# First operands by k over two queues, a bias wait at its first use, and another order around the last block's x1 and the sums

## The reference

```
h = rmsnorm(x, norm_mix_g)
z = gelu(h @ a_w_in);  u, v = split(z, 2)
v = rmsnorm(v, a_v_g)
s = per chunk of 128 tokens and group of 128 features: tril(w_s) @ v + b_s
x = x + (u * s) @ a_w_out
a = relu(rmsnorm(x, norm_mlp_g) @ mlp_w1)      # 4096 wide
x = x + (a * a) @ mlp_w2
out = rmsnorm(x, final_g)
```

## Time and profile before

| | |
|---|---|
| median of 3 runs | 1824.14 us (1823.81 to 1824.42) |
| the profiled execution | 1827.29 us |
| its span | 1825.5 us |
| busy, share of the span: PE, PEld, DVE, ACT, POOL | 99%, 82%, 61%, 43%, 22% |
| mean granted clock of TensorE | 0.996 |

### The profile page before, as it was taken

The page is one execution under the profiler, slowest core; times in us unless marked ns, Lnnn a source line. Parts: engine busy times, 40 slices in busy tenths (PEclk is TensorE's granted clock), DMA queues, the critical chain, the costliest instruction groups (busy, mean ns, idle before and its releaser), DMA issues.

```text
span 1825.5 us, 20165 instructions
## 1 busy us (share of the span) xinstructions
PE 1802.2 (99%) x8136; PEld 1497.9 (82%) x8136; DVE 1111.1 (61%) x1122; ACT 782.5 (43%) x880; POOL 407.1 (22%) x394
## 2 busy tenths in 40 slices
PE   9999999999999899999999999999999999999998
PEld 7888888888888788888878888878888888888886
DVE  3583483484384566654666655685666666866665
ACT  5553544434534533444543443354433335333333
POOL 2442442432340133310002111110234002000002
PEclk9999999999999899999999999999999999999999
DMA  8757656665655588875957777799977555854552
GB/s 329 269 209 267 240 215 241 244 244 204 234 199 201 199 290 267 303 263 183 355 197 237 259 256 229 278 367 319 309 299 264 220 202 201 288 184 185 199 205 103
DMA packets 134157, 445.40 MB, mean 244 GB/s; under 512 B 8112, under 2 KB 9136, under 8 KB 118320
## 3 DMA queue, kind: packets, MB, share of 16 engines
q1 hardware_dynamic: 105728, 329.02, 51.3%
q0 software_dynamic: 25168, 92.80, 14.3%
q10 hardware_dynamic: 3168, 22.30, 3.2%
HBM read 318.26 MB, written 125.83 MB: 243 GB/s over the span
## 4 chain that ended last, share of the span: by engine, by line
PE 92%; DVE 2%; DMA 2%; ACT 1%; SPq 1%; issue 1%; DVEq 0%; POOLq 0%; POOL 0%; ACTq 0%
PE bank L1263 62%; PE bank L1098 28%; DMA u_raw<-in_mlp_w 1%; PE bank L1144 1%; PE bank L1120 1%; SPq L312 1%; DMA bias_rows<-in_a_b_s 1%; PE bank L1147 0%; DMA x_raw<-xs 0%; DVE Y L1036 0%; ACT x_hi L581 0%; DVE x_lo L849 0%; DVE r L1017 0%; DVE sums L1020 0%; DVE u_lo L838 0%
## 5 line engine op out<-in xcount | busy, mean ns | idle before, releaser
L1263 PE MATMUL bank<-x_hi,u_hi 128*128 128x512 f32 x896 | 351.0, 392 | 8.0 <-ACT c L755 4.8
L1263 PE MATMUL bank<-x_lo,u_hi 128*128 128x512 f32 x896 | 349.9, 391 | 0.0
L1263 PE MATMUL bank<-x_hi,u_lo 128*128 128x512 f32 x896 | 349.8, 390 | 0.0
L1263 PE MATMUL bank<-d_lo,a_hi 128*128 128x512 f32 x896 | 348.9, 389 | 0.0
L1263 PE MATMUL bank<-d_hi,a_hi 128*128 128x512 f32 x896 | 348.9, 389 | 0.0
L1263 PE MATMUL bank<-d_hi,a_lo 128*128 128x512 f32 x896 | 348.9, 389 | 0.0
L838 DVE TENSOR_TENSOR u_lo<-u_raw,u_hi 128x1024 fp32r<-128x1024 f32 x112 | 148.9, 1329 | 180.2 <-ACT u_hi L571 180.2
L1007 DVE TENSOR_TENSOR Y<-bank,Y 128x512 f32<-128x512 f32 x208 | 138.0, 686 | 179.8 <-PE bank L1263 179.6
L576 ACT ACTIVATE d_hi<-d_raw 128x2048 fp32r<-128x2048 f32 x56 | 107.4, 1919 | 282.2 <-DMA d_raw<-w2sum 153.7
L832 DVE TENSOR_TENSOR w_lo<-w_raw,w_hi 128x2048 fp32r<-128x2048 f32 x47 | 116.5, 2490 | 171.5 <-ACT w_hi L566 160.5
L1263 PEld LDWEIGHTS bank<-x_hi,u_hi 128*128 128x128 f32 x896 | 168.9, 189 | 45.6 <-issue 8.4
(11 more groups left out here) (113 smaller groups left out, 2763.3 us busy)
## 6 DMA issues: line engine op xcount, KB each, us to landing
a_raw<-a2s SPq DMA_DIRECT2D x56, 1024.0 KB, 7.3
a2s<-sums SPq DMA_DIRECT2D x32, 1280.0 KB, 7.9
job<-in_mlp_w POOLq DMA_DIRECT2D x32, 1024.0 KB, 8.2
u_raw<-w1sum SPq DMA_DIRECT2D x64, 512.0 KB, 4.7
d_raw<-w2sum SPq DMA_DIRECT2D x32, 1024.0 KB, 4.9
w_raw<-in_a_w_in SPq DMA_DIRECT2D x31, 1024.0 KB, 5.9
u_raw<-in_mlp_w SPq DMA_DIRECT2D x48, 512.0 KB, 5.4
d_raw<-in_mlp_w SPq DMA_DIRECT2D x24, 1024.0 KB, 5.2
```

The source lines that it names most:

```text
L1263: ins = pe.matmul(bank_of(g, j)[:, :], stationary[x_part][:, k, j * P:(j + 1) * P], moving[y_part][:, k, :], start=i in (0, 1, 3) and k == ...
```

## The change

Unit 0's weights and the first four k-tiles of hT are loaded k by k, the weights on SP's queue, hT on ACT's (the gains behind the first k-tile); ACT, DVE and TensorE take them k by k. The warm-up has 44 transposes. DVE waits for the bias in the first `gate`. In ACT's loop `renew` comes before `finish_first` at i = 6, and behind `keep_x1T` at g = 4 and 5; the squares of the last x1 come at g = 1 behind `renew` instead of g = 0. DVE does `finish_second` for j = 0 at i = 0 in front of `renew`, and for j = 1 at i = 2 behind it, and SP stores these sums at i = 2 and 4. The other lines of the diff renumber semaphores, since unit 0 no longer counts in `w_hi_done`, `w_ready` and `w_loaded`.

```diff
-WARM = 48
+WARM = 44
...
-            for k in range(0, KU, 2):
-                rows = slice(k, k + 2)
-                to = (first_loaded[0], w_loaded[0])[k // 2]
-                sp.dma_start(w_raw[0][:, rows, :], w_in_v[:, rows, D:D + N]).then_inc(to, 16)
-                to = (first_loaded[1], xT_loaded[0])[k // 2]
-                sp.dma_start(hT_raw[0][:, rows, :], xT[0, 0][:, rows, :]).then_inc(to, 16)
+            for k in range(KU):
+                sp.dma_start(w_raw[0][:, k, :], w_in_v[:, k, D:D + N]).then_inc(first_w_loaded[k], 16)
...
-                if g >= STEPS and g % STEPS in (0, 1, 3, 5):
-                    part, j = {0: (0, 0), 1: (0, 1), 3: (1, 0), 5: (1, 1)}[g % STEPS]
+                if g >= STEPS and g % STEPS in (0, 1, 2, 4):
+                    part, j = {0: (0, 0), 1: (0, 1), 2: (1, 0), 4: (1, 1)}[g % STEPS]
...
-                    if q == 0 and k < 2:
-                        act.wait_ge(first_loaded[1], 16)
+                    if q == 0 and k < KU:
+                        act.wait_ge(first_h_loaded[k], 16)
                     else:
-                        act.wait_ge(xT_loaded[k // KU], 16 * (q + 1))
+                        act.wait_ge(xT_loaded[k // KU], 16 * (q if k < KU else q + 1))
...
+            act.dma_start(hT_raw[0][:, 0, :], xT[0, 0][:, 0, :]).then_inc(first_h_loaded[0], 16)
             act.dma_start(gains[:, :, :], gains_T).then_inc(gains_loaded, 16)
+            for k in range(1, KU):
+                act.dma_start(hT_raw[0][:, k, :], xT[0, 0][:, k, :]).then_inc(first_h_loaded[k], 16)
 
             act.wait_ge(half_done, 2)
             act.activation(junk[:, 0:2 * TT], minus_half[:, :], ACT.Copy).then_inc(warm, 1)
-            act.wait_ge(first_loaded[0], 16)
-            act.activation(w_hi[0][:, 0:2, :], w_raw[0][:, 0:2, :], ACT.Copy).then_inc(first_hi_done, 1)
-            act.wait_ge(gains_loaded, 16)
-            split_h(0, range(2))
-            act.wait_ge(w_loaded[0], 16)
-            act.activation(w_hi[0][:, 2:KU, :], w_raw[0][:, 2:KU, :], ACT.Copy).then_inc(w_hi_done, 1)
-            split_h(0, range(2, KD))
+            for k in range(KU):
+                act.wait_ge(first_w_loaded[k], 16)
+                act.activation(w_hi[0][:, k, :], w_raw[0][:, k, :], ACT.Copy).then_inc(first_hi_done, 1)
+                if k == 0:
+                    act.wait_ge(gains_loaded, 16)
+                split_h(0, range(k, k + 1))
+            split_h(0, range(KU, KD))
...
                     if i == 6:
+                        renew(g)
                         for j in range(2):
                             finish_first(c, j)
                     if i in (0, 2, 3, 6):
...
                             act.wait_ge(second_half, 6 * 2 * c)
                         for j in range(2):
                             keep_bank(g, j, to[:, j, :], ACT.Relu if i == 6 else ACT.Copy)
-                    renew(g)
-                    if g == 0:
-                        squares_x1(BLOCKS - 1)
                     if g == 4:
                         keep_x1T(BLOCKS - 1, 0)
                     if g == 5:
                         keep_x1T(BLOCKS - 1, 1)
+                    if i < 6:
+                        renew(g)
+                    if g == 1:
+                        squares_x1(BLOCKS - 1)
...
+                if q == 0 and g == 0:
+                    dve.wait_ge(bias_loaded, 16)
...
-            dve.wait_ge(first_hi_done, 1)
-            dve.tensor_tensor(w_lo[0][:, 0:2, :], w_raw[0][:, 0:2, :], f32(w_hi[0][:, 0:2, :]), ALU.subtract)\
-                .then_inc(first_ready, 1)
-            dve.wait_ge(gains_loaded, 16)
-            split_h(0, range(2))
-            dve.wait_ge(w_hi_done, 1)
-            dve.tensor_tensor(w_lo[0][:, 2:KU, :], w_raw[0][:, 2:KU, :], f32(w_hi[0][:, 2:KU, :]), ALU.subtract)\
-                .then_inc(w_ready, 1)
-            split_h(0, range(2, KD))
+            for k in range(KU):
+                dve.wait_ge(first_hi_done, k + 1)
+                dve.tensor_tensor(w_lo[0][:, k, :], w_raw[0][:, k, :], f32(w_hi[0][:, k, :]), ALU.subtract)\
+                    .then_inc(first_ready, 1)
+                if k == 0:
+                    dve.wait_ge(gains_loaded, 16)
+                split_h(0, range(k, k + 1))
+            split_h(0, range(KU, KD))
             split_w(1)
-            dve.wait_ge(bias_loaded, 16)
...
-                if c and i in (2, 3):
-                    finish_second(c - 1, i - 2)
+                if c and i == 0:
+                    finish_second(c - 1, 0)
                 renew(g)
+                if c and i == 2:
+                    finish_second(c - 1, 1)
...
-                if w == 0:
-                    pe.wait_ge(first_ready, 1)
-                else:
-                    pe.wait_ge(w_ready, w + 1)
+                if w:
+                    pe.wait_ge(w_ready, w)
                 for k in range(KU):
-                    if w == 0 and k == 2:
-                        pe.wait_ge(w_ready, 1)
+                    if w == 0:
+                        pe.wait_ge(first_ready, k + 1)
```

More of the change, by code:

```diff
@@ L175, in build @@
         mix_done, x1T_done = sem("mix_done"), sem("x1T_done")
-        first_loaded = [sem("first_w_loaded"), sem("first_h_loaded")]
+        first_w_loaded = [sem(f"first_w_loaded{k}") for k in range(KU)]
+        first_h_loaded = [sem(f"first_h_loaded{k}") for k in range(KU)]
         warm = sem("warm")
@@ L564, in split_w @@
             def split_w(w):
-                act.wait_ge(w_loaded[w % SLOTS], 16 * (w // SLOTS + 1))
+                act.wait_ge(w_loaded[w % SLOTS], 16 * (w // SLOTS + (1 if w % SLOTS else 0)))
                 act.activation(w_hi[w % SLOTS][:, :, :], w_raw[w % SLOTS][:, :, :], ACT.Copy)\
@@ L830, in split_w @@
                 s = w % SLOTS
-                dve.wait_ge(w_hi_done, w + 1)
+                dve.wait_ge(w_hi_done, w)
                 dve.tensor_tensor(w_lo[s][:, :, :], w_raw[s][:, :, :], f32(w_hi[s][:, :, :]), ALU.subtract)\
@@ L836, in split_u @@
                 s = g % SLOTS
[L837 removed]
+                dve.wait_ge(w_hi_done, FIRST + g)
                 dve.tensor_tensor(u_lo[s][:, :, :], u_raw[s][:, :, :], f32(u_hi[s][:, :, :]), ALU.subtract)\
@@ L1244, in _ @@
                     b = g // (UP // PAIRS * STEPS)
-                    pe.wait_ge(w_ready, FIRST + g + 1)
+                    pe.wait_ge(w_ready, FIRST + g)
                     pe.wait_ge(a_ready, b * STEPS + i + 1)
```

3 lines of the change are left out of this document (1 added, 2 removed).

## The result

| | before | after |
|---|---|---|
| median | 1824.24 us (4 runs, 1823.81 to 1824.42) | 1810.32 us (4 runs, 1809.70 to 1811.35) |
| ratio, with its 95% interval | | 0.9928 [0.9915, 0.9940] |
| the profiled execution | 1827.29 us | 1810.33 us |
| its span | 1825.5 us | 1808.6 us |
| mean granted clock of TensorE | 0.996 | 0.999 |

The kernel is faster by 13.9 us, 0.72%. Forecast were 19.1 us and 1805.0; the ratio puts the kernel at 1811.0 (0.9928 x 1824.14), the upper edge of the range. Between the two profiled executions it is 16.9 us. The interval is 2.3 us wide to either side, and those of the experiments are of that order.

What follows compares the result with a forecast made beforehand. TensorE was taken as the bound, with a few breaks: 2.35 + 11.1 + 0.45 + 4.45 + 1.75 = 20.1 us at most, less 1.0 for margins, 19.1; 1824.14 - 19.1 = 1805.0 us, range 1803.5 to 1811.

Steps and rivals of the forecast that it cites:

- The five places: The five breaks in TensorE's work that the change was to remove, together 20.1 us at most.
- Place 2: Steps 2 to 5 of the second stage (593.47 to 618.12): 10.25 us, with faster matmuls behind it 11.1 us.
- Places 3 and 5: Step 26 (733.37 to 733.81), 0.45 us, and steps 107 to 111 (1179.54 to 1203.08), 1.75 us: both losses go.
- the difference is applied to the median: Last step of the sum: 19.1 us, worked out on the profiled execution, taken from the median 1824.14 to give 1805.0.
- Place 1: First unit and bias wait (start to 32.80): unit 2 starts 2.15 us earlier, with slow first matmuls 2.35 us gained.
- behind a transfer that has the same bytes in front of it as before: Unit 1's w_lo, written from 17.26 to 19.55 as before, so unit 1 starts at 19.7 and not 20.23: 0.5 us.
- TensorE free at 8.55: End of the warm-up: four transposes less save 0.44 us, so TensorE is free at 8.55 instead of 8.98.
- Rival D: First unit starves: half-size pieces in two queues arrive later, unit 0 stops at each k; 1806 to 1809, chance 0.04.
- Place 4: Steps 54 to 61 (886.43 to 929.02): 4.45 us lost, all regained, or 2.4 if u_raw(57) lands no earlier.
- Rival C: DVE's full queue in steps 54 to 61 keeps 2.4 to 4.45 us: 1807 to 1809.5, chance 0.08.
- 5 us sooner: Steps 54 to 61: with j = 1 sums a step earlier, ACT's copy and x_hi(0) run 5 us sooner.
- The margins: 1.0 us taken off the 20.1 for margins of 0.05 to 0.4 us worked out with rounded durations.

Runs made afterwards that it cites:

- the second pair of profiles: The kernel before and the changed kernel, each run once more unchanged for a second profile: 1823.56 us (ratio 1.0003) and 1810.58 us (0.9927).
- the sums alone: The kernel before with only DVE's second-half sums and SP's stores of them moved earlier, ACT's loop unchanged: 1820.25 us, ratio 0.9976.
- The kernel without the start part: The changed kernel with unit 0 loaded in pairs of k on SP's queue and 48 warm-up transposes, as before the change: 1808.97 us, ratio 0.9917.
- the kernel with the late stores: The changed kernel with SP's stores of the second-half sums back at i = 3 and 5: 1811.99 us, ratio 0.9936.
- the one put together with them: The changed kernel with the old start, stores at i = 3 and 5, and x_raw(4) issued before the last x1 store: 1811.60 us, ratio 0.9936.

## Why the prediction was right and where it was wrong

- **Direction and places.** The five places were the right ones, and each is smaller or gone. Place 2, followed with the durations of the rows, came out at 10.22 for 10.25 in the profiled executions, with the clock at 1.00. That close a hit is in part luck: the second pair of profiles gives 7.2. Places 3 and 5 are gone, with the cause named, since they go with the sums alone.
- **From the profile to the median, 3.0 of the 5.2 us.** This is the step that cost most. For the profiled execution the sum was right to about 2 us: 1827.29 - 19.1 = 1808.2, measured 1810.33. Applied to the median it became 1805.0. The step "the difference is applied to the median" took 3 us for gained that the median, it seems, never lost: in steps 0 to 4 the four executions of the old order took 6.7 to 10.2 us more than the shortest of the new, 7.5 between the means, and the sum had entered the largest of these losses in full. That this accounts for the 3.0 us is argued from the traces of other executions, and not from one at the median.
- **Place 1, 2.35 forecast, 0.39 had.** The step that failed is that w_lo of unit 1 is written "behind a transfer that has the same bytes in front of it as before", and so at the same time. It started 1.3 us later: w itself landed 0.8 later, the second half of hT 0.7 later, and ACT had a fifth k-tile of hT in front of it. Of the 1.2 us that unit 2 still gains (it starts at 31.8 and not at 32.80, without slow matmuls) another 0.4 goes at 82.40, where the mix of block 0 waits, and some 0.2 in a slow matmul behind it; this wait is there in some traces with this start and not in others. The kernel without the start part has no such wait and keeps 1.9. Nor was TensorE free at 8.55: the warm-up doesn't shorten by 0.11 us for each transpose, for 44 took from 6.4 to 7.7 us and 48 from 7.0 to 8.3 in the traces. Rival D had the late pieces, with a chance of 0.04; but it looked for the harm at unit 0's k-tiles, where there is none, and not at unit 1. And it took 256 KB more or less as a question of bandwidth (1.3 us for 512 KB), while the engines idled.
- **Place 4, 4.45 forecast, 1.8 still waited.** Rival C named the point, that ACT's start hangs on the u loads and up to 2.4 us stay. I gave this 0.08, because the queue of DVE worked out in time with all data in time. It was another load than the one named. Against TensorE's step 54 u_raw(57) landed sooner, 883.4 - 874.1 = 9.3 us after it (874.1 is 607.51 + 49 x 5.44) instead of 897.5 - 886.4 = 11.1, but ACT stood for u_raw(56) until 882.18 and took up u_raw(57) at 884.96, 10.9 us after: no earlier. The failing term is ACT's start in that sum, "5 us sooner", for which the loads would have had to come sooner with the DMA engines full (0.96 to 1.03).
- **The margins.** Of the 1.0 us left for them step 4 takes 0 to 1.2, by the execution.

## What to carry to other kernels

Losses that depend on the landing of a DMA, and the falls of the clock behind them, differ from one execution to the next: measure them in several profiles before taking them from a median. A wait that is removed moves all work behind it against the engines that keep their own pace, so that one part of a change alone may bring less than its place and the whole more. Cutting the first loads into smaller pieces brought the first matmul forward by 1.2 us in the one kernel that also issued the gains first (8.16), and even there nothing was left at the second unit, whose data wait behind those pieces; so follow those.

## What was not expected of the hardware

- The clock at step 3: behind a wait of 2.02 to 2.03 us it fell from 1.00 to 0.50 (1.2 GHz) in two executions (24 matmuls in 7.34 and 7.35 us) and stayed in two others (5.75 and 5.73). What TensorE did before doesn't differ in their rows (72 matmuls in 16.32 us in all four). The fall is worth 1.6 us. It is the same at other places: in one and the same kernel, before, the clock stayed at 1.00 behind a wait of 3.41 us (at 929.02) in the first profile and fell to 0.50 behind one of 3.40 us (at 926.28) in the second. At step 59 it fell behind 2.16 us in the kernel with the late stores and stayed behind 2.15 us in the one put together with them (which had waited 1.84 us at 896.42 besides).
- The 1024 KB behind eight pieces of 256 KB in two queues landed at 13.3 us, and at 12.6 behind four of 512 KB in one, with the DMA share at 0.58 to 0.77 in between instead of 0.96 to 1.00.
- The same 48 transposes of the warm-up took 7.39 us in one kernel and 8.34 in another with the same start, and the 44 of after 7.59 us in its first profile and 6.89 in its second; what set this stays open.
